# A transformer layer on one core: W_in landed in place in full rows, output chains begun inside the last attention tiles, a new SBUF map

## The reference, cut to what matters

```python
mod = silu(c) @ w_ada + b_ada                      # six vectors of 1024
h = rmsnorm(x, norm1_gain) * (1 + scale1) + shift1
proj = h @ w_in                                    # 1024 x 1280: q | k | v | p
attn = sliding_window_attention(q, k, v, ...)      # window 128, T5 bias, learned sinks
pool = multiscale_pool(p, w_pool, pool_scale)      # windows 2, 4, 8, 16
merged = concat(rmsnorm(attn), rmsnorm(pool))
x = x + gate1 * (merged @ w_out)
h2 = rmsnorm(x, norm2_gain) * (1 + scale2) + shift2
x = x + gate2 * ((silu(h2 @ w_gate) * (h2 @ w_up)) @ w_down)
```

## Time and profile before

| | |
|---|---|
| time, median of 3 runs | 1127.53 us (1126.92 to 1132.89) |
| span of the profiled execution | 1128.6 us |
| PE busy | 1023.1 us (91%) |
| DVE, POOL, ACT busy | 465.4, 375.3, 276.2 us |
| chain that ended last, by engine | PE 74%, DVE 12%, POOL 5%, DMA 3%, issue 3%, ACT 2% |
| first matmul of the projection | at 67.4 us |
| rounds 0 to 9 of the loop | 67.4 to 273 us |
| output stage | 292.1 to 410.6 us |
| FFN | to the end |

### The profile page before, as it was taken

How to read it: one execution, slowest core, us unless ns; L and a number is a source line. 1 busy time by engine, 2 the same in 40 slices (tenths; PEclk the granted TensorE clock), 3 DMA queues, 4 the chain that set the end, 5 groups by cost and what they waited for, 6 DMA issues and landing times.

```text
span 1128.6 us, 12266 instructions
## 1 busy us (share of the span) xinstructions
PE 1023.1 (91%) x4716; PEld 845.1 (75%) x4716; DVE 465.4 (41%) x741; ACT 276.2 (24%) x511; POOL 375.3 (33%) x234
## 2 busy tenths in 40 slices
PE   2079999984599989999999999999999999999998
PEld 1058888773477768888888888888888888888887
DVE  5658889799545531230413122141312213141224
ACT  1225545445123332211111211111121111112010
POOL 1324564544923325331413132151323215132210
PEclk9579999987699999999999999999999999999999
DMA  8753452224621012202111030212103021211003
GB/s 286 261 179 115 145 168 97 94 93 157 238 91 56 19 35 77 87 26 75 38 56 57 1 100 13 74 37 74 37 0 111 0 74 37 74 37 37 0 0 150
DMA packets 67814, 93.32 MB, mean 83 GB/s; under 512 B 3280, under 2 KB 51136, under 8 KB 67776
## 3 DMA queue, kind: packets, MB, share of 16 engines
q1 hardware_dynamic: 62256, 80.82, 21.4%
q10 hardware_dynamic: 5520, 12.00, 3.1%
HBM read 84.02 MB, written 8.78 MB: 82 GB/s over the span
## 4 chain that ended last, share of the span: by engine, by line
PE 74%; DVE 12%; POOL 5%; DMA 3%; issue 3%; ACT 2%; SPq 0%; ACTq 0%; DVEq 0%; POOLq 0%
PE ps L1097 24%; PE ps L1099 23%; PE ps L1098 23%; DMA stage<-in_w_ada 3%; POOL wo_lo L698 2%; DVE xn L1029 2%; DVE acc L847 2%; DVE xn L902 1%; PE ps L1156 1%; POOL rs_qk L684 1%; DVE nmax L953 1%; DVE s_sb L952 1%; DVE x L1051 1%; DVE den L881 1%; DVE qn L994 1%
## 5 line engine op out<-in xcount | busy, mean ns | idle before, releaser
L1062 DVE TENSOR_TENSOR act_f<-silu_sb,ps 128x512 f32<-128x512 f32 x44 | 30.3, 688 | 393.0 <-PE ps L1099 379.0
L756 POOL TENSOR_TENSOR wg_lo<-raw_g,wg_hi 128x1024 fp32r<-128x1024 f32 x22 | 52.8, 2401 | 343.4 <-ACT wg_hi L567 343.4
L1074 DVE TENSOR_TENSOR x<-x,ps 128x512 f32<-128x512 f32 x176 | 120.9, 687 | 103.5 <-PE ps L1099 103.5
L1099 PE MATMUL ps<-h_hi,wu_lo 128*128 128x512 f32 x352 | 137.9, 392 | 0.0
L1098 PE MATMUL ps<-h_lo,wu_hi 128*128 128x512 f32 x352 | 137.8, 391 | 0.0
L1097 PE MATMUL ps<-h_hi,wu_hi 128*128 128x512 f32 x352 | 137.7, 391 | 0.0
L1097 PE MATMUL ps<-h_hi,wg_hi 128*128 128x512 f32 x352 | 137.2, 390 | 0.0
L1098 PE MATMUL ps<-h_lo,wg_hi 128*128 128x512 f32 x352 | 137.1, 390 | 0.0
L1099 PE MATMUL ps<-h_hi,wg_lo 128*128 128x512 f32 x352 | 137.1, 389 | 0.0
L1099 PE MATMUL ps<-wd_hi,act_lo 128*128 128x512 f32 x352 | 137.1, 389 | 0.0
L1098 PE MATMUL ps<-wd_lo,act_hi 128*128 128x512 f32 x352 | 137.1, 389 | 0.0
(11 more groups left out here) (155 smaller groups left out, 1673.3 us busy)
## 6 DMA issues: line engine op xcount, KB each, us to landing
stage<-in_w_ada SPq DMA_DIRECT2D x48, 512.0 KB, 5.7
raw_g<-in_w_gate SPq DMA_DIRECT2D x22, 512.0 KB, 3.6
...
```

Of the source, the lines that this page charges most:

```text
L756: pool.tensor_tensor(wgu[b][2 * s + 1][:, :, :], (raw_g, raw_u)[s][:, :, :], wgu[b][2 * s][:, :, :].bitcast(F32), ALU.subtract).then_inc(g ...
L1062: dve.tensor_tensor(act_f[:, :], silu_sb[:, :], bank(2 * n + 1), ALU.mult).then_inc(actf_done, 1)
L1074: dve.tensor_tensor(xt, xt, bank(4 + j % 4), ALU.add).then_inc(down_evac, 1)
L1099: return pe.matmul(dst, s_lo, m_hi, start=False, stop=stop)
```

## The change

The opening. `pieces` holds w_ada alone. Behind the 16 pieces of scale1 and shift1 SP issues W_in as eight full rows of 640 KB straight into `wi_raw`, with no slot to wait for; `wi_lo` overwrites `wi_raw` in place, POOL making the even k and DVE the odd. `acc` is doubled, so the folds of shift1 need not wait for the sum of scale1. The sums that end in columns are eight one-column matmuls (`sum_columns`) instead of full rows and a diagonal. Tile 0 is projected k by k, as the pieces come (`project_first`), and tile 1 is transposed inside it; `xn` is doubled, and ACT normalises tile 1 between its copies 4 and 5 of W_in. The table of 1/count lands in `pt_sb`.

The loop. `FOLDS` sets 5, 5, 5, 5, 4, 4, 4, 0 folds for rounds 0 to 7 and `SCALED` which rows of W_out are scaled there. W_out lands in `wo_raw` of its own. `wo_lo` is split between POOL (even) and DVE (odd). The rsqrt of the mixed rows (`rms_mix`) is taken tile by tile on POOL instead of once. `kT` keeps four chunks.

The end of the loop. ACT makes the eight `wo_hi` and splits mixed tile 0 ahead of its work of round 8. PE runs chain A of tile 0 at the head of round 9 and chain A of tile 1 inside it. In the output stage PE's order is A(t+1), B(t), transpose(t-1), and DVE's B-sum(t), A-sum(t+2), `h2_rows(t-1)`.

All buffers of SBUF have new, written-out addresses; the FFN's instructions are the same, and its first weight load is issued once two tiles of the output stage are summed.

```diff
-        pieces = [("ada", SCALE1, k) for k in range(KT)]
-        pieces += [p for k in range(KT) for p in (("ada", SHIFT1, k), ("in", k, 0))] + [("in2", n, 0) for n in range(2)]
-        pieces += [("ada", mm, k) for mm in BG for k in range(KT)]
-        pieces += [("out", k, 0) for k in range(KT)]
+        ADA = (SCALE1, SHIFT1, *BG)
+        pieces = [(mm, k) for mm in ADA for k in range(KT)]
+        FOLDS = (5, 5, 5, 5, 4, 4, 4, 0)
+        SCALED = ((), (), (), (), (0,), (1,), (2,), (3, 4, 5, 6, 7))
...
+        def out_banks(t, part):
+            return 0 if part == 0 and t >= 2 else 2
...
         @block.sync
+                if (mm, k) == (SHIFT1, KT - 1):
+                    for j in range(KT):
+                        sp.dma_start(wi_raw[:, j, :], win_d[j * P:(j + 1) * P, :]).then_inc(wi_in[j], 16)
+                if (mm, k) == (GATE1, KT - 1):
+                    for j in range(KT // 2):
+                        sp.dma_start(wo_raw[:, j, :], wout_d[j * P:(j + 1) * P, :]).then_inc(wo_in[j], 16)
...
+            sp.wait_ge(p_chain, NT)
+            load_mixed(0)
+            load_mixed(1)
...
         @block.scalar
+            for j in range(KT):
+                act.wait_ge(wi_in[j], 16)
+                act.activation(wi_hi[:, j, :], wi_raw[:, j, :], ACT.Copy).then_inc(wi_hi_done, 1)
+                if j == 4:
+                    norm_x(1)
...
             for it in range(NT + 2):
+                if it == NT:
+                    act.wait_ge(p_chain, NT)
+                    for k in range(KT // 2):
+                        wo_high(k)
+                    split_m(0)
+                    for k in range(KT // 2, KT):
+                        wo_high(k)
+                if it == NT + 1:
+                    split_m(1)
...
         @block.gpsimd
             rms_x(0)
+            wi_low(0)
             h_high(0)
+            wi_low(2)
+            wi_low(4)
             rms_x(1)
+            wi_low(6)
             pool.wait_ge(const_in, 16 * 7)
...
+                if it == NT:
+                    wo_low(0)
+                    wo_low(2)
+                    m_low(0)
+                    wo_low(4)
+                if it == NT + 1:
+                    wo_low(6)
+                    m_low(1)
...
+                if 1 <= z:
+                    rms_mix(z - 1)
...
         @block.vector
             h_rows(0)
+            wi_low(1)
             h_low(0)
+            wi_low(3)
+            wi_low(5)
+            wi_low(7)
...
+                if it == NT - 1:
+                    wo_low(1)
+                    wo_low(3)
+                if it == NT:
+                    wo_low(5)
+                    wo_low(7)
+                    mixed_sum(0, 0)
...
+            mixed_sum(1, 0)
+            for t in range(NT):
+                mixed_sum(t, 1)
+                if t + 2 < NT:
+                    mixed_sum(t + 2, 0)
                 if t >= 1:
                     h2_rows(t - 1)
...
         @block.tensor
+            def project_first():
+                for k in range(KT):
+                    pe.wait_ge(wi_lo2_done if k % 2 else wi_lo_done, k // 2 + 1)
+                    for dst, cols, done in (...):
+                        last = mm3(dst, ht_hi[:, 0, k, :], ht_lo[:, 0, k, :], wi_hi[:, k, cols], wi_lo[:, k, cols],
+                                   k == 0, k == KT - 1)
+                    if k == 5:
+                        transpose_x(1, -1)
...
+                if it == NT + 1:
+                    pe.wait_ge(mlo_done, 1)
+                    pe.wait_ge(wo_lo_done, KT // 4)
+                    pe.wait_ge(wo_lo2_done, KT // 4)
+                    out_chain(0, 0)
...
+                if it == NT + 1:
+                    pe.wait_ge(mlo_done, 2)
+                    pe.wait_ge(x1a_done, 1)
+                    out_chain(1, 0)
...
+            pe.wait_ge(x1a_done, 2)
+            out_chain(0, 1)
             sum_squares(NT - 1)
...
+            for t in range(1, NT):
+                if t + 1 < NT:
+                    pe.wait_ge(mlo_done, t + 2)
+                    if t >= 2:
+                        pe.wait_ge(x1a_done, t + 1)
+                    out_chain(t + 1, 0)
+                pe.wait_ge(x1_done, t)
+                out_chain(t, 1)
+                transpose_x2(t - 1)
```

More of the change, by code:

```diff
@@ L114, in build_program @@
         mhalf = sb("mhalf", [P, 16])
[L117 to L165, removed]
@@ new lines, in place, with row_of @@
+        def place(name, shape, offset, dt=F32):
+            return nc.alloc_sbuf_tensor_at(name, shape, dt, offset=offset)
+        def row_of(offset, *rows):
+            made = []
+            for name, shape in rows:
+                made.append(place(name, shape, offset))
+                offset += -(-math.prod(shape[1:]) * 4 // 32) * 32
+            return made
+        KB = 1024
+        BASE = nc.sbuf_base
+        RAW = BASE + 96 * KB
+        XIN = RAW + 32 * KB
+        MIX = XIN + 16 * KB
@@ new lines, in build_program @@
+        m_raw = place("m_raw", [P, KT, SEQ], BASE + 32 * KB)
+        h_lo = place("h_lo", [P, KT, SEQ], BASE + 32 * KB, F32R)
+        wo_hi = place("wo_hi", [P, KT, D], BASE + 64 * KB, F32R)
+        wo_raw = place("wo_raw", [P, KT, D], RAW)
+        wo_lo = place("wo_lo", [P, KT, D], RAW, F32R)
+        x1 = place("x1", [P, NT, D], XIN)
+        xn2 = place("xn2", [P, D], GU)
+        raw_g = place("raw_g", [P, KT, P], GU + 4 * KB)
+        raw_u = place("raw_u", [P, KT, P], GU + 8 * KB)
+        wgu = [[place(f"w{n}{b}", [P, KT, P], GU + (12 + 16 * b + 4 * j) * KB, F32R)
+                for j, n in enumerate(("g_hi", "g_lo", "u_hi", "u_lo"))] for b in range(2)]
@@ L228, in build_program @@
         ada_used = sem("ada_used")
+        wi_in = [sem(f"wi_in{k}") for k in range(KT)]
         wi_hi_done = sem("wi_hi_done")
@@ L231, in build_program @@
         wi_lo2_done = sem("wi_lo2_done")
+        wo_in = [sem(f"wo_in{k}") for k in range(KT)]
         wo_scaled = sem("wo_scaled")
+        wo_lo2_done = sem("wo_lo2_done")
         wo_hi_done = sem("wo_hi_done")
@@ L761, in low_gu @@
                 low_part(f, b, 1)
[L763 to L771 removed]
+            m_low(2)
+            rms_mix(NT - 1)
             for t in range(NT):
@@ L915, in _ @@
             for k in range(KT):
-                fold(SCALE1, k)
+                fold(k)
                 if k == KT // 2:
                     small_vectors()
-            take(SCALE1, (7, 5))
+            take(SCALE1, (7,))
             gain_columns(a1, 0, N1)
```

403 lines of the change are left out of this document (183 added, 220 removed).

## The result

The changed kernel takes 1143.6 us (median, 1141.8 to 1144.9) where the kernel before takes 1128.2 us on the same chip: the ratio is 1.0128, with a 95% interval of 1.0104 to 1.0151. It is slower by 1.3%; the forecast of 1127 us, no measurable change, was wrong. Its profiled execution has a span of 1140.0 us against 1128.6.

A forecast was written before the change was run, and what follows sets the result against it. Time was lost ahead of the FFN: the W_in wait, PE and DVE taking turns, and W_out's low parts with the output stage. -11 + 4 + 3 + 3.4 = -0.6 gave 1127 us, range 1111 to 1139 (8 in 10).

The forecast's parts named there:

- The forecast sum: Whole kernel: opening -11, loop +4, end and output stage +3, clock +3.4, together -0.6 us.
- the ring: Output stage: DVE's A-sum ahead of h2_rows waits for a chain behind PE's transposes; 14.7 us a tile instead of 12.9.
- The clock: Output stage: two of six chains behind waits fall to half clock at 1.7 us each, +3.4, bounds 0 and +16.
- Rival 2: Output stage: each wait cools PE, every chain starts at half clock, +10 to +16, 1133.5 to 1139.5 us; chance 0.26.
- the rule alone: Output stage: by the skill's page, waits between bursts bring half clock back at every burst; time 1139.5 us.
- The output stage's tile: Output stage: 14.7 us a tile instead of 12.9, PE idle 2.9 of them.
- End of the loop: ACT reaches round 8 at 265 us instead of 250.4; with the output stage +3 us, from -2 to +7.
- The loop: Rounds of the loop: folds 3.6, round 6 -1.2, rms_mix 1.6; +4 us, from 0 to +7.
- The term for folds: Loop: a fifth fold costs 0.4 us in an odd and 1.4 in an even round, two each: 3.6 us.
- `rms_mix`, for which I took 1.6: Loop: new rsqrt on POOL costs between 0 and one 0.69-us instruction in five rounds; half taken, 1.6 us.
- The opening: Before the loop: W_in lands sooner, PE starts tile 1 at 71.7 instead of 84.4 us; -11, bounds -17 and -7.
- The lockout of DVE and POOL: Opening and loop's end: a shared port fully blocks the loser, so splitting low parts over both engines gives no overlap.

The follow-up runs named there:

- e2: Changed kernel plus 12 throwaway matmuls in PE's wait ahead of the transposes of tiles 1 to 5: 1136.69 us.
- f4: Kernel before with only DVE's output-stage order changed to B-sum(t), A-sum(t+1), h2_rows(t-1): 1145.04 us, ratio 1.0144.
- e4: Changed kernel with the loop's folds dealt out as 4, 4, 4, 4, 5, 5, 5, 1: 1142.55 us.
- e1: Changed kernel with DVE doing h2_rows(t-1) ahead of the A-sum of tile t+2 in the output stage: 1119.96 us, ratio 0.9921.
- f1: Kernel of e1 with PE's attention of the last tile ahead of chain A(1) instead of behind it: 1108.83 us.
- e3: Changed kernel with ACT's seven DMAs of small constants issued ahead of the W_in copies: 1139.64 us.
- f2: Changed kernel with h2_rows ahead of the A-sum, last attention ahead of A(1), constants ahead of W_in copies, tile 1's normalisation behind them: 1106.72 us, ratio 0.9805.
- f3: Kernel of e3 with tile 1's normalisation on ACT behind the last W_in copy instead of the fifth: 1138.30 us.
- g3: Kernel of f2 with DVE's reading of scale1's sum moved behind shift1's fourth fold: 1106.63 us.
- g2: Kernel of f2 with four folds in each of eight rounds and all eight scalings of W_out in round 7: 1108.96 us.

## Why the prediction was wrong, step by step

The forecast sum was -0.6 and the two traces differ by +11.4. The 12.0 us between them are, in round numbers, 4.4 in the opening, 2.4 in the loop, 2.5 at its end, 1.0 in the ring without the clock, 3.1 in the clock of the output stage, and -1.6 at the start of the FFN.

- **The clock: the failed step.** "I count two of six at 1.7", so +3.4. All five chains behind such a wait ran cold at first, 6 to 8 matmuls each, at 1.6 us a tile: 6.5 us from the first transposes to the last (99.3 us, in e2 92.8). Chain A(1) ran cold as well and took 8.1 us instead of 5.5. Together that is 9 us where I had 3.4. Rival 2 was the case, with its mechanism, near the low end of its +10 to +16. I gave it 0.26, and leaned on rows 6 against it. One of them I misread: I took the transposes of 1.09 us at 409.53 for slow ones. They take that at the full clock behind any wait (f4 at 332.99); the slow matmuls stand behind them (PE, timeline, kernel before):

```profile
409.53 1.09 PE L1251 MATMUL ps<-ident,xn 128*128 128x128 f32 x8 [4.09 <-ACT xn L611]
...
411.11 0.63 PE L1099 MATMUL ps<-h_hi,wu_lo 128*128 128x512 f32 x1
```

  So the trace of before has two waits of PE in this stage behind its first chain, of 2.77 us (at 303.41) and of 4.09, and eight slow matmuls behind each: two of two, where I counted one and set it aside because its forerunner had been cold. The changed kernel's first wait of 2.81 us, behind 27 us at the full clock, answers that argument. By the Trainium skill, "TensorE: Matmul & The Clock Gate", section "HAM oscillation — how this bites in real kernels", the half clock comes back at every burst; this trace agrees for all five chains, those of e4 and f4 from the second on. By the rule alone I had 1139.5 us, the nearest of my figures.
- **The output stage's tile: the mechanism right, the size short.** The ring I described is the one in the trace, and f4 and e1 show by either sign that it is the cause. I had it at 14.7 us; without the clock it takes 15.3 to 15.7 (e2). The steps up to `xn2` sum to 8.1 us (348.01 to 356.12 in e2; I had 8.25). Missing were POOL's low part of the mixed tile, which lets the chain start 0.2 us behind the transposes, and 0.4 us of the chain, which takes 5.9 us to its A-sum (357.43 to 363.30) and not 5.5. The split of the FFN's weights costs 0.4 us in two tiles; there I had too much, 1.05 each. Over the whole stage the misses nearly cancel: 92.8 us in e2 against my 91.8.
- **End of the loop: right, in part by luck.** First scores at 273.27 us (273), A-sum(0) at 287.8 (288.3). But ACT's start of round 8, 265 us, was the middle of two bounds; in the trace it is at 265.65 because ACT waits 12.5 us in all for DVE's scalings, which begin at 254.40 and take 2.05 us each. B(0) came at 304.5 instead of 301.3, since A(1) ran cold. I took the last attention's place behind A(1) as given; f1 shows that it cost 11 us.
- **The loop: +6.4 instead of +4.** Rounds 1 to 5 came out 0.4 shorter and then 1.7, 2.6, 1.7 and 0.9 us longer. The term for folds was mis-sized: a fifth operation costs 1.7 us in rounds 2 and 4 and next to nothing in round 1, not 0.4 behind an odd and 1.4 behind an even round (e4). POOL's windows running beside the folds are my reading of it; no run tests them apart. `rms_mix`, for which I took 1.6, costs 0 in the round that shows it. The rest are two rounds with a lower clock, of 26.1 us instead of 25.2. In e3 all rounds from tile 3's on took 25.2; in f2, with the same loop, two took 26.4 and 26.8. So this part is 0 to 3 us and changes from kernel to kernel with nothing in the loop changed.
- **The opening: -6.6 instead of -11, the second failed step.** Over all traces it is nearer -3. The constants did become the wait, landing at 71.8 us (66.6). The eight one-column matmuls cost 3.7 us and not 1.7, twice; shift1's folds ended at 38.8 instead of 32.7 as its folds came 1.5 to 4.0 us apart and not 1.45. ACT stood 8.9 us in tile 1's normalisation until POOL came to `rsx`, and three copies waited behind it. Tile 0 so began at 51.67 us instead of 44 and took the 17 us I had given it. Taking the constants' wait away gave about 4 us (e3), the copies' and the sum's waits nothing that can be told: PE works on tile 0 without a gap meanwhile (f3), and the DMA sets the pace of the folds (g3).
- **The lockout of DVE and POOL: right.** Beside POOL's low parts DVE's of a row of W_in took 4.2 us in place of 1.5 and that of h 3.9 in place of 1.2, and the scalings of g2 are the clearest case. The Trainium skill's page "SBUF — State Buffer", section "SBUF: two separate sides", has the loser of the shared port blocked for the other's whole instruction; the trace agrees, with these numbers: POOL's low part ends at 54.33 us, and DVE's, begun at 51.49, 1.35 us later, about its own length. I read it as what makes the end of the loop a fixed sum; g2 fits, and no run tests it apart.

Left open: why the first wait of a series lowers the clock in one kernel and not in another, and why the same wait of 2.05 us for `s_sb` in the loop is followed by a granted clock of 0.50 and 0.73 in the next two windows of 4 us in the changed kernel, and of 0.63 and 0.95 in e3.
